# Fused transformer blocks in split-float32: rotation steps one earlier, output splits spread over heads, up-projection weights split ahead, pooling sums moved among the projection blocks

## What is computed

```python
# layer 0: retention, 4 heads, q/k 256 wide, v 512 wide
q, k = apply_rope(q), apply_rope(k) / 16
o = decayed scores(q, k) @ v;  o = rms_norm(o) * silu(g);  x += gate * (o @ w_out)
# layer 1: chunked attention, 16 heads of 128, each query sees 5 tiles of keys at most
p = softmax(q k^T * scale + bias);  x += gate * ((p @ v) * silu(g)) @ w_out
# layer 2: four average pools (windows 2, 4, 8, 16) beside latent attention, 8 heads
y_pool = ((window mean - u) @ pool_w) * pool_scale * silu(g_pool)
q = rmsnorm(q_lat) @ w_uq;  k_nope, v = rmsnorm(kv_lat) @ w_ukv;  q, k = rope(rmsnorm(q)), rope(rmsnorm(k))
x += gate * (concat(y_pool, softmax(q k^T) v * silu(g_attn)) @ w_out)
```

## Time and profile before

| | us |
|---|---|
| median of 3 runs | 2827.83 (2826.27 to 2830.09) |
| the profiled execution's own time | 2828.05 |
| its span, first to last instruction | 2826.2 |
| PE busy | 2643.7 (94%) |
| DVE busy | 1692.3 (60%) |
| ACT busy | 1025.1 (36%) |
| POOL busy | 917.8 (32%) |

### The profile page before, as it was taken

How to read it: one execution, slowest core, us unless ns; L and a number is a source line. 1 busy time by engine, 2 the same in 40 slices (tenths; PEclk the granted TensorE clock), 3 DMA queues, 4 the chain that set the end, 5 groups by cost and what they waited for, 6 DMA issues and landing times. The chain is left out here.

```text
span 2826.2 us, 40714 instructions
## 1 busy us (share of the span) xinstructions
PE 2643.7 (94%) x16444; PEld 2284.4 (81%) x16444; DVE 1692.3 (60%) x2410; ACT 1025.1 (36%) x1709; POOL 917.8 (32%) x670
## 2 busy tenths in 40 slices
PE   5999999989999989999999999998999994899998
PEld 5888999856578889999998877776888872788887
DVE  6877677545434389876675456665334656665544
ACT  4322223211134332222223356665343333555551
POOL 1555455300034454554555510000443553000014
PEclk9999999999999999999999999999999997799999
DMA  6454534742024324432423374440342432000023
GB/s 232 128 174 172 176 127 166 243 166 90 23 89 142 113 101 164 139 112 91 127 90 107 118 208 139 117 126 18 127 149 90 149 130 77 7 1 1 1 75 142
DMA packets 241414, 328.12 MB, mean 116 GB/s; under 512 B 19134, under 2 KB 178110, under 8 KB 239436
## 3 DMA queue, kind: packets, MB, share of 16 engines
q1 hardware_dynamic: 239756, 325.42, 34.5%
q10 hardware_dynamic: 1472, 0.10, 0.0%
HBM read 246.16 MB, written 79.33 MB: 115 GB/s over the span
## 5 line engine op out<-in xcount | busy, mean ns | idle before, releaser
L793 POOL TENSOR_TENSOR w_lo<-raw,w_hi 128x512 fp32r<-128x512 f32 (+1 forms) x614 | 888.7, 1455 | 1856.3 <-ACT w_hi L1238 1855.7
L1238 ACT ACTIVATE w_hi<-raw 128x512 fp32r<-128x512 f32 (+1 forms) x614 | 378.8, 628 | 1114.6 <-PE ps L833 876.0
L831 PE MATMUL ps<-w_hi,s_hi 128*128 128x256 f32 (+1 forms) x1344 | 383.0, 285 | 12.6 <-POOL w_lo L793 12.6
L832 PE MATMUL ps<-w_lo,s_hi 128*128 128x256 f32 (+1 forms) x1344 | 381.3, 284 | 0.0
L833 PE MATMUL ps<-w_hi,s_lo 128*128 128x256 f32 (+1 forms) x1344 | 381.1, 284 | 0.0
L831 PE MATMUL ps<-w_hi,a_hi 128*128 128x256 f32 (+1 forms) x1008 | 287.7, 285 | 10.6 <-DVE a_lo L1596 8.8
L832 PE MATMUL ps<-w_lo,a_hi 128*128 128x256 f32 (+1 forms) x1008 | 287.4, 285 | 0.0
L833 PE MATMUL ps<-w_hi,a_lo 128*128 128x256 f32 (+1 forms) x1008 | 287.3, 285 | 0.0
L1640 DVE TENSOR_TENSOR u<-u,ps 128x1024 f32<-128x1024 f32 (+1 forms) x128 | 155.3, 1214 | 216.8 <-PE ps L833 212.9
L831 PEld LDWEIGHTS ps<-w_hi,s_hi 128*128 128x128 f32 x1344 | 259.2, 193 | 23.6 <-issue 22.6
L833 PEld LDWEIGHTS ps<-w_hi,s_lo 128*128 128x128 f32 x1344 | 259.5, 193 | 0.0
(11 more groups left out here) (265 smaller groups left out, 5485.3 us busy)
## 6 DMA issues: line engine op xcount, KB each, us to landing
raw<-in_w SPq DMA_DIRECT2D x207, 512.0 KB, 3.9
ada_c<-in_ada SPq DMA_DIRECT2D x14, 2304.0 KB, 10.9
blk<-u SPq DMA_DIRECT2D x62, 512.0 KB, 3.4
blk<-c SPq DMA_DIRECT2D x31, 512.0 KB, 3.4
blk<-m1s SPq DMA_DIRECT2D x31, 512.0 KB, 3.4
ada_first<-in_ada SPq DMA_DIRECT2D x12, 768.0 KB, 16.1
r_g<-blk SPq DMA_DIRECT2D x8, 1024.0 KB, 11.8
r_v<-blk SPq DMA_DIRECT2D x4, 2048.0 KB, 11.5
```

What stands on the lines that cost most here:

```text
L793: pool.tensor_tensor(w_ring(w_lo, n), w_source(n), w_ring(w_hi, n).bitcast(F32), ALU.subtract)\
L831: pe.matmul(out, a_hi_, b_hi_, start=first, stop=False, skip_group_check=True)
L832: pe.matmul(out, a_hi_, b_lo_, start=False, stop=False, skip_group_check=True)
L1238: act.activation(w_ring(w_hi, n), w_source(n), ACT.Copy).then_inc(w_rounded, 1)
```

## The change

Seven things are altered.

- **Rotation.** The steps of the next retention head are at units 0 to 5 of a head and not 1 to 6. Those of head 0 are two each at points 0, 1 and 2 of block 11, where all six were at point 3; its loads are issued at block 10 and no more at block 11. One modulation piece moves for that: `ADA_BLOCKS` loses block 10 and gains block 17.
- **Output splits of attention.** The five early pairs are one each in heads 4, 6, 8, 10, 12 (ACT at unit 5, DVE at unit 6).
- **Block order.** LU is block 28 and LAT block 29; SP's loads of the two are exchanged.
- **Pooling sums.** `windows` runs for pool 1 at point 3 of block 29, pools 0 and 3 at points 0 and 1 of block 30, pool 2 at point 1 of block 31. The squares of the latents are at (30, 3) and (31, 0), their scaling at (31, 2), ACT's root at (31, 2).
- **Up-projection weights.** All six slots are rounded and split right after the last projection. Their low halves go over their raw weights (`up_lo`), the high halves of slots 4 and 5 into `w_lo`. SP reloads those raw buffers when the last up-projection is done.
- **Key rotation.** POOL rotates all eight tiles after the six slots.
- **Turned keys.** `l_klhi` and `l_kllo` are at 4 and 8 KiB. PE turns the first two latent tiles after the eviction of c21, and only the third waits for c12; ACT evacuates without the wait for the stores, and its two Sin instructions come behind the evacuations.

The diff, without context and with the indentation shortened:

```diff
@@ -54 +54 @@
-LAT, LU, LGP, LGA = 28, 29, 30, 31
+LU, LAT, LGP, LGA = 28, 29, 30, 31
@@ -104 +104 @@
-ADA_BLOCKS = (*range(1, 11), *range(13, 17))
+ADA_BLOCKS = (*range(1, 10), *range(13, 18))
@@ -225,2 +225,2 @@
-l_klhi = place("l_klhi", 112, [P, S], F32R)
-l_kllo = place("l_kllo", 116, [P, S], F32R)
+l_klhi = place("l_klhi", 4, [P, S], F32R)
+l_kllo = place("l_kllo", 8, [P, S], F32R)
@@ -228,0 +229 @@
+up_lo = [place(f"up_lo{n}", 144 + 4 * j, [P, 2, 512], F32R) for n, j in enumerate((R11, R12, R22))]
@@ -358,0 +360,2 @@
@@ -359,0 +363,4 @@
+    if kind[0] == "U":
+        if ring is w_lo:
+            return up_lo[kind[1] // 2][:, kind[1] % 2]
+        return (w_hi if kind[1] < 4 else w_lo)[:, n % RING]
@@ -499 +506 @@
-        sp.wait_ge(n_turned, 16 if n < 10 else 32)
+        sp.wait_ge(n_turned, 16 if n < 9 else 32)
@@ -648 +655 @@
-        sp.wait_ge(m_acc, 10)
+        sp.wait_ge(m_acc, 9)
@@ -676 +683 @@
-    projections(0, {11: r_first}, r_after)
+    projections(0, {10: r_first}, r_after)
@@ -748 +755 @@
-        def l_first():
+        def l_second():
@@ -750 +756,0 @@
-            sp.wait_ge(n_turned, 48)
@@ -751,0 +758,6 @@
+        def l_first():
+            in_memory(LU)
+            sp.wait_ge(n_turned, 48)
+            for n in range(4):
+                sp.dma_start(l_u[:, n, PAD:PAD + S], rows_of(LU)[n * P:(n + 1) * P, :]).then_inc(l_uin[n], 16)
@@ -758,5 +769,0 @@
-        def l_second():
-            in_memory(LU)
-            for n in range(4):
-                sp.dma_start(l_u[:, n, PAD:PAD + S], rows_of(LU)[n * P:(n + 1) * P, :]).then_inc(l_uin[n], 16)
@@ -778,0 +786 @@
+        sp.wait_ge(w_used, UP[5] + 1)
@@ -780 +787,0 @@
-            sp.wait_ge(w_split, UP[0] + 2 * n + 2)
@@ -785 +792 @@
-    sp.wait_ge(m_st, 16 * (14 if LAST else 10))
+    sp.wait_ge(m_st, 16 * (14 if LAST else 9))
@@ -818,3 +824,0 @@
-        if LAST == 2 and n == UP[4]:
-            for m in range(6):
-                key_rope(m)
@@ -822 +826 @@
-            for m in range(6, NT):
+            for m in range(NT):
@@ -1098 +1102 @@
-        pe.wait_ge(ev, evicted(31, "c12"))
+        pe.wait_ge(ev, evicted(31, "c21"))
@@ -1100,0 +1105,2 @@
+            if n == 2:
+                pe.wait_ge(ev, evicted(31, "c12"))
@@ -1107 +1112,0 @@
-            pe.wait_ge(l_diff, n + 1)
@@ -1108,0 +1114 @@
+                pe.wait_ge(l_diff, 4)
@@ -1122,4 +1128,2 @@
-            if u == 0:
-                pe.wait_ge(w_split, UP[1] + 1)
-            if u == NT:
-                pe.wait_ge(w_split, UP[5] + 1)
+            if u in (0, NT):
+                pe.wait_ge(w_split, UP[1 if u == 0 else 5] + 1)
@@ -1129,3 +1133,3 @@
-                    n = UP[c] % RING
-                    mm = product(ps[:, bank + c], l_klhi[:, tok], l_kllo[:, tok], w_hi[:, n], w_lo[:, n],
-                                 True, True)
+                    n = UP[c]
+                    mm = product(ps[:, bank + c], l_klhi[:, tok], l_kllo[:, tok], w_ring(w_hi, n),
+                                 w_ring(w_lo, n), True, True)
@@ -1134 +1138 @@
-                        n = UP[2 + 2 * c + k] % RING
+                        n = UP[2 + 2 * c + k]
@@ -1136,5 +1140,3 @@
-                                     w_hi[:, n, 0:384], w_lo[:, n, 0:384], k == 0, k == 1)
-            if u == NT - 1:
-                mm.then_inc(w_used, 2)
-            elif u == 2 * NT - 1:
-                mm.then_inc(w_used, 4)
+                                     w_ring(w_hi, n)[:, 0:384], w_ring(w_lo, n)[:, 0:384], k == 0, k == 1)
+            if u == 2 * NT - 1:
+                mm.then_inc(w_used, 6)
@@ -1236 +1238,3 @@
-        if n >= RING:
+        if kind[0] == "U":
+            act.wait_ge(w_used, min(n - RING + 1, UP[0]))
+        elif n >= RING:
@@ -1290 +1294,2 @@
-            act.wait_ge(a_odone, NT * (AH if a or kp >= 5 else AH - 1))
+            if a or kp >= 5:
+                act.wait_ge(a_odone, NT * AH)
@@ -1469,2 +1474,2 @@
-            if h == AH - 1 and 2 <= i < 2 + O_EARLY[1]:
-                o_round_pair(1, 0, i - 2)
+            if h % 2 == 0 and i == 5 and 4 <= h < 4 + 2 * O_EARLY[1]:
+                o_round_pair(1, 0, h // 2 - 2)
@@ -1476 +1481 @@
-            if (s, i) == (30, 6):
+            if (s, i) == (31, 2):
@@ -1483,4 +1488 @@
-        act.wait_ge(rope_reduced, 4)
-        act.activation(sin2[:, :, :], sin2[:, :, :], ACT.Sin).then_inc(rope_tables, 1)
-        act.activation(cos2[:, :, :], cos2[:, :, :], ACT.Sin).then_inc(rope_tables, 1)
-        for n in range(2, 4):
+        for n in range(2, 6):
@@ -1488,2 +1489,0 @@
-        for c in QUADS:
-            act.wait_ge(stored[c], 16 * 32)
@@ -1494,0 +1495,4 @@
+        act.wait_ge(rope_reduced, 4)
+        act.activation(sin2[:, :, :], sin2[:, :, :], ACT.Sin).then_inc(rope_tables, 1)
+        act.activation(cos2[:, :, :], cos2[:, :, :], ACT.Sin).then_inc(rope_tables, 1)
@@ -1502,3 +1506 @@
-            if u == NT - 1:
-                act.wait_ge(w_used, UP[1] + 1)
-            elif u == 2 * NT - 1:
+            if u == 2 * NT - 1:
@@ -1507 +1509 @@
-                act.wait_ge(l_updone, u + (1 if u < NT else 0))
+                act.wait_ge(l_updone, u + 1)
@@ -1519,3 +1521,2 @@
-            if u == NT - 1:
-                for n in range(4, 6):
-                    hi(UP[n])
+                for c in QUADS:
+                    act.wait_ge(stored[c], 16 * 32)
@@ -1892,3 +1893,3 @@
-        if (s, point) == (11, 3):
-            for n in range(6):
-                r_rope_step(0, n)
+        if s == 11 and point < 3:
+            r_rope_step(0, 2 * point)
+            r_rope_step(0, 2 * point + 1)
@@ -1937,2 +1938,2 @@
-        if h + 1 < RH and 1 <= i < 7:
-            r_rope_step(h + 1, i - 1)
+        if h + 1 < RH and i < 6:
+            r_rope_step(h + 1, i)
@@ -1992,2 +1993,2 @@
-            if h == AH - 1 and 2 <= i < 2 + O_EARLY[1]:
-                o_split_pair(1, 0, i - 2)
+            if h % 2 == 0 and i == 6 and 4 <= h < 4 + 2 * O_EARLY[1]:
+                o_split_pair(1, 0, h // 2 - 2)
@@ -2001,0 +2003 @@
+        pooled = {(29, 3): 1, (30, 0): 0, (30, 1): 3, (31, 1): 2}
@@ -2004,3 +2006 @@
-            if point != 3:
-                return
-            if s == 29:
+            if (s, point) == (29, 0):
@@ -2010 +2010,5 @@
-            if s == 30:
+            if (s, point) in pooled:
+                windows(pooled[s, point], list(pooled).index((s, point)))
+            if (s, point) in ((30, 3), (31, 0)):
+                n = s - 30
+                lo, width = lat_parts[n]
@@ -2012,7 +2016,6 @@
-                for n, (lo, width) in enumerate(lat_parts):
-                    part = l_lat[:, :, lo:lo + width]
-                    sq = lat_sq[:, 0:NT * width].rearrange("p (m n) -> p m n", m=NT)
-                    link(dve.tensor_tensor(sq, part, part, ALU.mult), l_chain)
-                    dve.tensor_reduce(st[:, 8 * n:8 * n + 8], sq, AX.X, ALU.add).then_inc(l_sums, 1)
-                    dve.wait_ge(l_sums, n + 1)
-            if s == 31:
+                part = l_lat[:, :, lo:lo + width]
+                sq = lat_sq[:, 0:NT * width].rearrange("p (m n) -> p m n", m=NT)
+                link(dve.tensor_tensor(sq, part, part, ALU.mult), l_chain)
+                dve.tensor_reduce(st[:, 8 * n:8 * n + 8], sq, AX.X, ALU.add).then_inc(l_sums, 1)
+                dve.wait_ge(l_sums, n + 1)
+            if (s, point) == (31, 2):
@@ -2025,2 +2027,0 @@
-                for n in range(2):
-                    windows(n)
@@ -2028 +2029 @@
-        def windows(n):
+        def windows(n, before):
@@ -2032 +2033 @@
-            dve.wait_ge(l_consts, 16 * 6)
+            dve.wait_ge(l_consts, 16 * 5)
@@ -2051 +2052 @@
-            dve.wait_ge(l_diff, n + 1)
+            dve.wait_ge(l_diff, before + 1)
@@ -2068,0 +2070,2 @@
+        lat_low(0)
+        dve.wait_ge(l_consts, 16 * 6)
@@ -2081,2 +2083,0 @@
-        lat_low(0)
-        windows(2)
@@ -2087 +2087,0 @@
-        windows(3)
```

4 lines of the change are left out of this document (2 added, 2 removed).

## The result

The changed kernel takes 2759.82 us (median of 4 runs, 2759.33 to 2760.69), the kernel before, on the same chip, 2828.96. The ratio is 0.9754, with a 95% interval of 0.9737 to 0.9771. The forecast of 2758.0 and its range hold it.

The account below looks back on a forecast made before the run. PE, busy 94% of the span, bounds the kernel, so only its waits and slow work after them can be gained. Terms 22 + 6 + 9 + 34 - 1 = 70 us off 2828.05 give 2758; range 2744 to 2782.

Parts of the forecast that it names:

- Rotation, heads 1 to 3: Retention: rotation steps one unit earlier remove three PE waits of about 5.6 us and slow matmuls behind them; 22 us gained.
- Head 0: Retention's first head: loads taken from in front bring the store of c21, and PE's scores, forward; 6 us gained.
- Attention: Output pairs leave the last head, 13 us gained, and cost 4 us in heads 4 to 12; net 9 us.
- Rival B: Side gains fail: first head stays bound by the store, pairs cost the same in five heads; 2773 us, chance 0.15.
- Pool sums: Layer 2 preparation: 22 us of DVE pool sums on the path move to blocks 29 to 31, at cost 0.
- Rival C: Pools stay on the path: late evictions cost 3 to 5 us in each of three blocks; 2770 us, chance 0.06.
- Start of the key units: Layer 2 preparation: DVE's first key sum comes near 2350.3, 20.4 us earlier.
- Query units: Layer 2 preparation: without PE's wait for a weight split, queries start 39.2 us earlier on DVE.
- Collision: Layer 2 preparation: DVE's query rotations meet POOL's key rotations in four units more than before; 5 us lost.
- Modulation in block 17: The piece moved there from block 10 adds one PE wait for a split, 1.9 us as bound; 1 us lost.
- Rival A: Keys end last: POOL ends 12 us later, PE's first head starts 3 to 6 us late; 2763 us, chance 0.16.
- Rival D: Slower: PE waits for all moved work and then works slowly, 58 + 25 = 83 us lost; 2841 us, chance 0.03.

Follow-up runs that it names:

- the base: The changed kernel run once more without edits, beside three of the other runs on the same chip: 2759.6 us.
- the late gates: Changed kernel with ACT's rounding of two retention output-weight slots behind block 11's Silus, and gate loads of heads 1 and 2 behind its last stores: 2753.47 us.

## Why the prediction was right

- **Rotation, heads 1 to 3: 22 forecast, 22.6 in the traces, 26 in the medians when undone.** Right, down to the slow value matmuls; 2.1 us of the difference arose in head 0.
- **Head 0: 6 forecast, 4.9 to the same scores; 7.0 when counted from c11 of block 1, 5.7 from the end of the projections.** The size was right, its reason half. That the store of c21 held TensorE and that fewer loads ahead of it would help, held. That the chain ran over ACT, which waited 18.2 us for a raw weight, did not: with that wait taken from in front of the Silu the store landed no earlier than the spread of the base. Both waited for the same full DMA engines, as the gain from the late gates says. How much of the head's gain is the spread rotation and how much the earlier loads was not separated.
- **Attention: 9 forecast, 9.7 in the traces, 11.3 in the medians.** The two halves were off in opposite ways: together the pairs cost 15.0 us where I had 13, and apart 1.05 each where I had 0.8. That their difference came out so near is luck in part. Rival B, which needs both this and the last point to fail, is out.
- **Pool sums: forecast at nothing.** Two of them undone cost 13.7 us, as the arithmetic of the earlier trace rows has it. The layer 2 projections took 1.5 us more, which may look like cover that was missing, but with two of the sums taken out again they took no less. Rival C's 3 to 5 us a block did not come.
- **Start of the key units: 20.4 earlier forecast.** VectorE's first key sum was at 2319.09, 51.7 us before 2370.79, of which 32.6 came from ahead: 19.1. The turned keys were ready when forecast (5.6 us behind the last projection product); VectorE's chain from there to the sum took 18.0 us, where I had worked out 16.3. Of the 1.7 us between, 1.1 are the first instruction of the angles, which now runs beside GpSimd's last split and took 0.17 before (and 0.16 with the key rotations first, where the splits end ahead of it); 0.5 are an idle place in front of the sum:

```profile
2302.34 1.27 DVE L2073 CAST l_fr<-st 128x8 f32<-128x8 int32 x1
```

- **Query units: 39.2 earlier forecast, 37.7 measured.** VectorE's first query sum was at 2406.69 before, 78.5 us behind the last projection product, and at 2336.36 after, 40.8 behind.
- **Collision: 5 us more than before forecast, 5.2 measured.** From that sum to the first turned query it was 2430.26 - 2406.69 = 23.6 us before and 28.8 after. The whole collision is 8.2 us (no key rotations), 6.8 of it in the query units, 2 us in a full one and not 1.3, but in three full ones and a part and not in more: number and price were off in opposite ways. The price was too low because I had it from the small products of the earlier trace rows and left out the scaling of a whole tile.
- **"PE's idle 10.8 us before the first head stays"** was wrong as a statement on TensorE: it is 20.6. The time of the head was right all the same, since VectorE sets it.
- **The slow stretch behind the waits before the first latent head was left out.** From the first turned query to the end it took 2.7 us less, all of it up to the second head (21.8 us before, 19.1 after). The granted clock (third number from the end; 0.50 is the lower of its two levels, 1.00 the upper) over the first 20 us, before:

```profile
2430.00:2440.00 10.00, 7.22 (x25) 5.92 (x26) 3.35 (x4) 3.50 (x3) 0.00 (x0) 0.50 0.00 0
2440.00:2450.00 10.00, 9.67 (x33) 7.39 (x31) 5.96 (x11) 4.80 (x7) 0.00 (x0) 0.55 0.00 0
```

and in the changed kernel:

```profile
2365.00:2375.00 10.00, 7.35 (x28) 5.94 (x28) 4.03 (x5) 4.01 (x4) 0.00 (x0) 0.67 0.00 0
2375.00:2385.00 10.00, 9.66 (x53) 7.75 (x52) 6.79 (x12) 5.32 (x8) 0.00 (x0) 0.77 0.00 0
```

- **Modulation in block 17: 1 forecast, 1 to 3 measured.** Waits for `w_lo` from 1200 us to 1240 us (blocks 17 and 18), where one wait of 1.1 us stood before. My text names 1.9 us as the bound, and the low end of the sum takes 3:

```profile
PE ps L835 <- POOL w_lo L800: 2.9, 2, 1.9
```

- **Rival A** had its rule right and its end wrong. The SBUF — State Buffer page of the Trainium skill (section "SBUF: two separate sides") says that the shared port pair is an exclusive lock for a whole instruction. The rows of the second query rotation agree: 1.37 us for 0.24 beside 1.47 of GpSimd, and 0.59 for 0.46 on GpSimd's side. But VectorE loses more (2.0 us a unit, GpSimd 0.24 a tile), as one would expect where GpSimd's instructions are the longer ones, and it ended at 2365.0, GpSimd's keys 8.8 us before. **Rival D** (moved work lands on TensorE's path) shows at no more than 3.1 + 1.5 us instead of 83.
- **The sign "first head turned near 2394"** does not follow from the terms, which give 2430.26 - 34 = 2396; measured was 2365.13 + 32.6 = 2397.7.

The total was nearer than the terms: 22.6 + 4.9 + 9.7 + 32.5 + 2.7 - 3.1 - 1.5 = 67.8, where the slow clock, not counted on, made up for a good half of what the projections lost. With the 2.1 us of chance at c11 of block 1 set aside it would be 69.9, and the medians differ by 69.1. That it lies within 1 us of the 70 forecast is luck in part, since the errors of the pairs, of the collision and of the projections have opposite signs. Left open: about half of the 3.1 us in layer 1, which of the moves costs the 1.5 us in layer 2 (the sums of pools 2 and 3 do not), and what lengthens the wait for r_s from one execution to the next. The new home of the turned keys and the exchange of the two blocks were not tried by themselves.

## What to carry to other kernels

A stall that comes back at the same unit of a loop went here by moving each step of the helper one unit earlier, at no cost that shows; look at what else starts at that unit first. Spreading work that stalls a loop is not free either: each part keeps a price of its own, here 1.05 us a pair against 3 us a pair in one place. When an engine waits for a store, read the time from its issue to its landing before blaming the engine that released the issue: here it was 11.3 us, and 4.7 of them went when 3 MB of loads that nobody needed yet were moved behind it. And when VectorE and GpSimd are put side by side, price every instruction of the one by the longest of the other that it can meet; only VectorE's sums and its evictions out of PSUM kept their time beside GpSimd here.
